# Folding the norm into a linear attention: the new x's sum of squares put together from three sums, and x updated in pairs of tiles

## What is computed

```python
# end of first_block
h = rms_norm(x, norm_ffn_pre_g[l])
f = (jax.nn.silu(h @ w_gate[l]) * (h @ w_up[l])) @ w_down[l]
x = x + rms_norm(f, norm_ffn_post_g[l])
# start of second_block
mod = (cond @ w_ada[l] + b_ada[l])[:, None, :]
sh1, sc1, g1, sh2, sc2, g2 = jnp.split(mod, N_MOD, axis=-1)
h = rms_norm_2(x, norm1_g[l]) * (1 + sc1) + sh1
proj = h @ w_in[l]
gq, gk, gv, gr, glr, aq, ak, av = jnp.split(proj, split_at, axis=-1)
```

## Time and profile before

| | |
|---|---|
| Median of 3 runs | 1440.65 us (1437.36 to 1441.19) |
| The profiled execution | 1441.32 us, of which its span is 1439.3 us |
| PE busy | 1390.4 us, 97% of the span |
| DVE busy | 882.9 us, 61% |
| ACT busy | 590.0 us, 41% |
| Share of the chain that ended last | PE 90%, DVE 5%, ACT 2% |
| DMA moved | 146.72 MB, 102 GB/s on average |

### The profile page before, as it was taken

One profiled execution on the slowest core, in us unless ns is written; L12 is line 12 of the kernel. 1 busy time (PEld: TensorE's weight loads), 2 busy tenths in 40 slices (PEclk: granted clock), 3 DMA queues, 4 the chain that ended last, 5 costly groups with the idle time before them and its releaser, 6 DMA issues.

```text
span 1439.3 us, 18374 instructions
## 1 busy us (share of the span) xinstructions
PE 1390.4 (97%) x6330; PEld 1098.6 (76%) x6330; DVE 882.9 (61%) x1450; ACT 590.0 (41%) x966; POOL 70.5 (5%) x128
## 2 busy tenths in 40 slices
PE   7999999999999999999997999899989999999999
PEld 5777777767768888888884788677668888888887
DVE  5666677777567777774336688666556656655222
ACT  5455445543352323323224524466445444444221
POOL 4000000000001221211000000000000000000000
PEclk9999999999999999999998999999999999999999
DMA  5222212213216565565431122021112232223332
GB/s 186 100 73 74 74 59 78 77 54 114 99 44 201 187 196 192 187 195 160 136 109 59 44 74 74 30 74 59 55 60 77 97 102 87 102 96 107 103 95 84
DMA packets 42319, 146.72 MB, mean 102 GB/s; under 512 B 5392, under 2 KB 5664, under 8 KB 42272
## 3 DMA queue, kind: packets, MB, share of 16 engines
q1 hardware_dynamic: 34448, 120.39, 25.5%
q0 software_dynamic: 7824, 25.70, 5.4%
HBM read 143.97 MB, written 2.10 MB: 101 GB/s over the span
## 4 chain that ended last, share of the span: by engine, by line
PE 90%; DVE 5%; ACT 2%; issue 1%; DMA 0%; DVEq 0%; ACTq 0%
PE bank L598 62%; PE bank L713 12%; PE bank L670 3%; PE bank L633 3%; PE bank L735 2%; PE bank L754 1%; PE bank L923 1%; PE bank L772 1%; ACT w_hi L1079 1%; PE bank L620 1%; DVE w_lo L1549 1%; PE bank L639 1%; DVE gate_last L1739 0%; DVE gate_a L1739 0%; PE bank L775 0%
## 5 line engine op out<-in xcount | busy, mean ns | idle before, releaser
L1549 DVE TENSOR_TENSOR w_lo<-raw,w_hi 128x1024 fp32r<-128x1024 f32 (+1 forms) x225 | 272.2, 1212 | 176.1 <-ACT w_hi L1079 175.3
L1079 ACT ACTIVATE w_hi<-raw 128x1024 fp32r<-128x1024 f32 (+1 forms) x225 | 233.6, 1039 | 302.8 <-PE bank L598 282.0
L598 PE MATMUL bank<-h_hi,w_hi 128*128 128x512 f32 x872 | 346.3, 397 | 0.8 <-DVE gyf L2045 0.8
L598 PE MATMUL bank<-h_hi,w_lo 128*128 128x512 f32 x872 | 340.6, 391 | 0.0
L598 PE MATMUL bank<-h_lo,w_hi 128*128 128x512 f32 x872 | 340.5, 391 | 0.0
L598 PEld LDWEIGHTS bank<-h_hi,w_hi 128*128 128x128 f32 x872 | 164.2, 188 | 42.5 <-issue 7.7
L598 PEld LDWEIGHTS bank<-h_hi,w_lo 128*128 128x128 f32 x872 | 164.3, 188 | 34.6
L598 PEld LDWEIGHTS bank<-h_lo,w_hi 128*128 128x128 f32 x872 | 164.4, 188 | 34.2 <-issue 1.2
L598 PE MATMUL bank<-f_hi,w_lo 128*128 128x512 f32 x352 | 136.9, 389 | 0.0
L598 PE MATMUL bank<-f_hi,w_hi 128*128 128x512 f32 x352 | 136.9, 389 | 0.0
L598 PE MATMUL bank<-f_lo,w_hi 128*128 128x512 f32 x352 | 136.9, 389 | 0.0
(11 more groups left out here) (299 smaller groups left out, 1867.7 us busy)
## 6 DMA issues: line engine op xcount, KB each, us to landing
raw<-in_w_up SPq DMA_DIRECT2D x66, 512.0 KB, 3.2
raw<-in_w_mix SPq DMA_DIRECT2D x48, 512.0 KB, 3.2
ada<-in_w_ada POOLq DMA_DIRECT2D x96, 256.0 KB, 3.2
raw<-in_w_down SPq DMA_DIRECT2D x32, 512.0 KB, 3.5
raw<-in_w_in SPq DMA_DIRECT2D x25, 512.0 KB, 3.3
raw<-in_w_gate SPq DMA_DIRECT2D x22, 512.0 KB, 3.3
raw<-in_w_out SPq DMA_DIRECT2D x16, 512.0 KB, 3.3
raw<-in_w_down SPq DMA_DIRECT2D x16, 384.0 KB, 3.3
```

The costliest lines, as they stand in the source:

```text
L598: last = pe.matmul(to[:, :], wt[:, slot, k, :], act_[:, rhs0 + k, :], start=(k == first and n == 0), stop=(k == K - 1 and n == 2))
L1079: act.activation(w_hi[:, s, 0:K, :], raw[:, s, 0:K, :], ACT.Copy).then_inc(hi_ready[s], 1)
L1549: dve.tensor_tensor(w_lo[:, s, 0:K, :], raw[:, s, 0:K, :], w_hi[:, s, 0:K, :].bitcast(F32), ALU.subtract).then_inc(split_ready[s], 1)
```

## The change

The sum of squares of the new x is no longer taken from the new x. With f the down product, g its gain and r its inverse root, x_new = x + r*g*f, and so

sum(x_new^2) = sum(x^2) + 2 r sum(x*g*f) + r^2 sum((g*f)^2).

The first sum is in bank S0 since the feed-forward norm. The other two are gathered while the down projection runs: per output tile ACT writes `oT` with the gain in it and squares it with the gain (`gained_tile`, three operations in place of two), and DVE makes one product and two additions more (`add_cross`). PE adds three sums over the first seven tiles between the second and third slot of the last output tile (`sums_so_far`, one of them in place of the one after the last product) and three over the last tile behind it (`last_sums`). DVE puts the sums together in four operations, ACT makes the second inverse root of them, and DVE then updates x two tiles at a time (two operations on 1024 elements per pair) between the modulated tiles (`modulated_with_update`). `post_norm` is no longer called here, nor are `new_x_squares` and `sum_squares_by_tile`. The last pair of output tiles is written out of the loop on PE. `split_lo(2)` and the clearing of `gacc` with its `m2_free` stand behind `modulated_with_update`; before, they stood between `post_norm` and `modulated_lo`.

```diff
-        (oT,), _ = region(h_at, ("oT", [KD, S], F32))
+        (oT, cross, cross_sum, gained_sq), h_end = region(
+            h_at, ("oT", [KD, S], F32), ("cross", [2, S], F32), ("cross_sum", [2, S], F32), ("gained_sq", [2, S], F32))
+        assert h_end <= h_at + 2 * KD * S * 4
...
-            def sum_squares_by_tile():
-
-                for k in range(KD):
-                    pe.wait_ge(sq_g[k % 2], w.next(sq_g[k % 2]))
-                    pe.matmul(S0[:, :], ones[:, :], sq[:, k % 2, :], start=(k == 0),
-                              stop=(k == KD - 1)).then_inc(sq_used[k % 2] if k < KD - 1 else ms_ready, 1)
-                for g in range(2):
-                    w.skip(sq_used[g], 4)
...
-            def down(read):
+            def sums_so_far():
+
+                w.skip(sq_g[0], 4)
+                w.skip(sq_used[1], 4)
+                pe.wait_ge(sq_used[0], w.next(sq_used[0], times=4))
+                pe.matmul(S1[:, :], ones[:, :], sqacc[:, :], start=True, stop=False)
+                pe.wait_ge(gained_used[0], 5)
+                pe.wait_ge(gained_used[1], 4)
+                for m in range(2):
+                    pe.matmul(TB[m][:, :], ones[:, :], cross_sum[:, m, :], start=True, stop=False)
+
+            def last_sums():
+
+                pe.wait_ge(sq_g[1], w.next(sq_g[1], times=4))
+                pe.matmul(S1[:, :], ones[:, :], sq[:, 1, :], start=False, stop=True).then_inc(ms_ready, 1)
+                pe.wait_ge(gained_sq_r[1], 4)
+                pe.matmul(T1[:, :], ones[:, :], gained_sq[:, 1, :], start=False, stop=True)
+                pe.wait_ge(cross_r, 1)
+                pe.matmul(T0[:, :], ones[:, :], cross[:, 1, :], start=False, stop=True).then_inc(cross_ms, 1)
+
+            def down(read, sums=None):
                 pe.wait_ge(f_ready, w.next(f_ready, times=NF - 1))

-                def pair(late=None):
+                def pair(late=None, sums=None):
                     for g in range(2):
                         pe.wait_ge(read[g], w.next(read[g], ahead=1))
                         unit(OB[g], 1, f_hi, f_lo, rhs0=8, K=NF)
                         unit(OB[g], 0, f_hi, f_lo, K=NF, first=-1)
+                        if g and sums:
+                            sums()
                         products(OB[g], 2, f_hi, f_lo, 0, 6, rhs0=16, K=6, first=-1,
                                  late=None if g else late).then_inc(unit_done[2], 1)

                 pair(f_ready)
-                with w.repeat(3, {**{split_ready[s]: 2 for s in range(3)}, (read[0], 1): 1, (read[1], 1): 1}):
+                with w.repeat(2, {**{split_ready[s]: 2 for s in range(3)}, (read[0], 1): 1, (read[1], 1): 1}):
                     pair()
+                pair(sums=sums)

             for g in range(2):
                 pe.wait_ge(g_free[g], 23)
             two_tiles(m_hi, m_lo, drained, 3, fresh=mix_ready)
             sum_squares()
             ffn(gate_read, up_read, True)
-            down(drained)
-            sum_squares()
-
-
-            sum_squares_by_tile()
+            down(drained, sums_so_far)
+            last_sums()
+
+
             two_units((S1, G1), (1, 0))
...
+            def gained_tile(g, c):
+
+                gain = col("norm_ffn_post_g", c)
+                act.wait_ge(gained_used[g], w.next(gained_used[g], ahead=1))
+                act.wait_ge(sq_used[g], w.next(sq_used[g], ahead=1))
+                act.activation(sq[:, g, :], OB[g][:, :], ACT.Square).then_inc(sq_g[g], 1)
+                act.activation(oT[:, bass.ds(c, 1), :].rearrange("p a s -> p (a s)"), OB[g][:, :], ACT.Identity,
+                               scale=gain).then_inc(gained[g], 1)
+                act.activation(gained_sq[:, g, :], OB[g][:, :], ACT.Square, scale=gain).then_inc(gained_sq_r[g], 1)
+                act.wait_ge(gained_sq_r[g], w.next(gained_sq_r[g]))
+                act.sem_inc(drained[g], 1)
...
-            down(lambda g, c: out_tile(g, c, oT, OB))
-            inverse_rms()
+            down(gained_tile, {(gained_used[0], 1): 1, (gained_used[1], 1): 1, gained_sq_r[0]: 1, gained_sq_r[1]: 1})
+            inverse_rms(sums=S1)
             split_hi(2)
-            new_x_squares()
-
-
-            inverse_rms()
+            act.wait_ge(ms2_ready, 1)
+            then(act.activation(sqacc[:, :], sqacc[:, :], ACT.Ln, scale=1.0 / D, bias=eps6[:, :]))
+            act.activation(sqacc[:, :], sqacc[:, :], ACT.Exp, scale=-0.5).then_inc(rstd2_ready, 1)
             modulated_hi(lambda k: mod_a[:, 0, k:k + 1], lambda k: modc[:, k:k + 1])
...
+            def modulated(k, root):
+
+                dve.wait_ge(h_ready, w.next(h_ready, ahead=2))
+                dve.tensor_tensor(hbuf[:, k % 2, :], xT[:, k, :], root[:, :], ALU.mult).then_inc(xr_ready, 1)
+
+            def remainder(k):
+
+                dve.wait_ge(n_hi, w.next(n_hi))
+                dve.tensor_tensor(h_lo[:, k, :], hbuf[:, k % 2, :], h_hi[:, k, :].bitcast(F32),
+                                  ALU.subtract).then_inc(h_ready, 1)
+
             def modulated_lo():

                 dve.wait_ge(rstd_ready, w.next(rstd_ready))
-
-                def lo(k):
-                    dve.wait_ge(n_hi, w.next(n_hi))
-                    dve.tensor_tensor(h_lo[:, k, :], hbuf[:, k % 2, :], h_hi[:, k, :].bitcast(F32),
-                                      ALU.subtract).then_inc(h_ready, 1)
-
                 for k in range(KD):
-                    dve.wait_ge(h_ready, w.next(h_ready, ahead=2))
-                    dve.tensor_tensor(hbuf[:, k % 2, :], xT[:, k, :], rstd[:, :], ALU.mult).then_inc(xr_ready, 1)
+                    modulated(k, rstd)
                     if k >= 1:
-                        lo(k - 1)
-                lo(KD - 1)
+                        remainder(k - 1)
+                remainder(KD - 1)
+
+            def modulated_with_update():
+
+                def updated(j):
+                    pair = slice(2 * j, 2 * j + 2)
+                    then(dve.tensor_tensor(oT[:, pair, :], oT[:, pair, :], rstd[:, :].rearrange("p (a s) -> p a s", a=1)
+                                           .broadcast_to([P, 2, S]), ALU.mult))
+                    then(dve.tensor_tensor(xT[:, pair, :], xT[:, pair, :], oT[:, pair, :], ALU.add))
+
+                dve.wait_ge(rstd_ready, w.next(rstd_ready))
+                dve.wait_ge(cross_ms, 1)
+                then(dve.tensor_tensor(sqacc[:, :], T1[:, :], rstd[:, :], ALU.mult))
+                then(dve.scalar_tensor_tensor(out=sqacc[:, :], in0=T0[:, :], scalar=2.0, in1=sqacc[:, :], op0=ALU.mult,
+                                              op1=ALU.add))
+                then(dve.tensor_tensor(sqacc[:, :], sqacc[:, :], rstd[:, :], ALU.mult))
+                dve.tensor_tensor(sqacc[:, :], sqacc[:, :], S0[:, :], ALU.add).then_inc(ms2_ready, 1)
+                updated(0)
+                dve.wait_ge(rstd2_ready, 1)
+                modulated(0, sqacc)
+                modulated(1, sqacc)
+                for j in range(1, 4):
+                    updated(j)
+                    for k in (2 * j, 2 * j + 1):
+                        remainder(k - 2)
+                        modulated(k, sqacc)
+                remainder(KD - 2)
+                remainder(KD - 1)

...
+            then(dve.memset(cross_sum[:, :, :], 0.0))
+
+            def add_cross(g, c):
+
+                dve.wait_ge(gained[g], w.next(gained[g]))
+                then(dve.tensor_tensor(cross[:, g, :], at_k(xT, c), at_k(oT, c), ALU.mult))
+                then(dve.tensor_tensor(cross_sum[:, 0, :], cross_sum[:, 0, :], cross[:, g, :], ALU.add))
+                dve.wait_ge(gained_sq_r[g], w.next(gained_sq_r[g]))
+                dve.tensor_tensor(cross_sum[:, 1, :], cross_sum[:, 1, :], gained_sq[:, g, :], ALU.add).then_inc(gained_used[g], 1)
+
+            def last_cross():
+
+                skip_last_square()
+                dve.wait_ge(gained[1], w.next(gained[1]))
+                dve.tensor_tensor(cross[:, 1, :], xT[:, 7, :], oT[:, 7, :], ALU.mult).then_inc(cross_r, 1)
+
             def square_and_modulation(g, c):

                 add_squares(g)
+                add_cross(g, c)
...
-            post_norm(oT, lambda k: col("norm_ffn_post_g", k))
+            modulated_with_update()
             split_lo(2)
             dve.memset(gacc[:, :, :], 0.0).then_inc(m2_free, 1)


-            modulated_lo()
             for n in (2, 3, 4):
```

More of the change, by code:

```diff
@@ L1324, in _ @@
             out_tile(1, 7, oT_mix, G)
-            def new_x_squares():
-                for k in range(KD):
-                    act.wait_ge(x_ready, w.next(x_ready))
-                    square(k, xT[:, k, :])
             inverse_rms()
@@ L1356, in _, with down @@
             w.start(unit_done, "down")
-            def down(each):
+            def down(each, more):
                 split_hi(2, K=6)
                 per = {**{raw_in[s]: 2 for s in range(3)}, **{(unit_done[s], 1): 2 for s in range(3)}, unit_done[2]: 2,
-                       (sq_used[0], 1): 1, (sq_used[1], 1): 1}
```

(1 more changed line is left out.)

25 lines of the change are left out of this document (15 added, 10 removed).

## The result

The changed kernel takes **1446.36 us** (median of 7 runs, 1445.41 to 1447.03) against 1441.19 (median of 7, 1437.36 to 1442.87) for the kernel before: +5.2 us, a ratio of 1.0035, 95% interval 1.0024 to 1.0046. The profiled execution took 1445.6 us, 1443.7 of it span. The median is 1.3 us above the forecast of 1445.1. The prediction took 0.3% as what can be told from no change: the ratio is just beyond that, and its interval reaches across it.

What follows compares the result with a forecast made beforehand. PE, busy 97%, bounds, with a near-equal ACT and DVE path from 801.72 to 826.74 us. Of loads 16.7 us late 4.1 come through: 1445.4 from the execution's 1441.3, 1444.8 from the median, written 1445.1; range 1443.5 to 1447.5.

Steps and rivals of the forecast that it cites:

- First combining operation: DVE, behind the down projection: the last tile's sums can be read, and combining starts, at 774.0 us.
- The three sums: PE, end of the down projection: three sums ahead of the last slot, with no pause to cover them, +2.58 us.
- GLA products: PE, GLA projection: products begin at 784.0 us, 4.6 us earlier, then wait for tiles that come every 2.6 us.
- Last remainder: DVE, end of update and modulation: the last remainder starts at 797.9 us, behind ACT's work on the last tile.
- The update's pace: DVE, update and modulation: each of three further pairs takes 5.18 us, together 15.5 us, to 796.1.
- `m2_free`: DVE's clearing of `gacc`, now behind the update: comes at 801.9 in place of 785.2 us, 16.7 us later, holding SP's loads.
- Tile 2 at ACT: ACT's rounding of tile 2 waits for its late load until 805.8 us, where it started at 801.72: +4.1 us.
- Small products: PE, GLA stage: start at 830.8 us, 826.74 plus 4.1, after a pause of 2 to 3 us.
- the rival with a lost clock: PE pauses before `z` (gate product; 2.5 us slack) and small products: half clock costs 2.2 us; 1447.3 us, chance 0.15.
- Both clock rivals: Same delay: clock given back near 920 us, 3 us back, 1442.1, chance 0.25; or clock lost, 1447.3, chance 0.15.
- The faster rival: Loads in time, and the GLA products' 4.6 us earlier start reaches the end; 1436.1 us, chance 0.08.
- The slow update: DVE's update: an operand repeated over two tiles halves the rate, 4.9 us more in all; 1450 us, chance 0.05.

Runs made afterwards that it cites:

- e3: The changed kernel with SP's load of `wgate` issued ahead of its wait for `m2_free`, the tiles still behind it; 1447.02 us, ratio 1.0044 to the kernel before.
- e4: The kernel before with only the split of tile 1 and the clearing of `gacc` moved behind `modulated_lo`; 1444.21 us, ratio 1.0021.
- e7: The changed kernel with four more sums on PE filling its pause ahead of `z`, the gate product; 1450.17 us, ratio 1.0048 to the kernel before.
- e1: The changed kernel with the clearing of `gacc` (and its `m2_free`) put ahead of `modulated_with_update`; 1439.77 us, ratio 0.9988 to the kernel before.
- e10: e1 with the three early sums moved behind the last product and the inverse-root scaling left out for tiles 2 to 7; 1435.71 us, ratio 0.9963.
- e1 to e3: e1, e3 and, between them, the changed kernel with loads of tiles 2 and 3 issued before SP's wait for `m2_free`: 1446.83 us, ratio 1.0037.
- e12: The same kernel as e1, run on another chip; 1441.60 us, ratio 1.0006 to the kernel before.
- e8: e6 with the scaling and addition that update x for tiles 4 to 7 moved from DVE to GpSimd; 1443.04 us, ratio 1.0006.
- e6: e1 with `gacc` cleared by GpSimd, behind DVE's last cross product, in place of DVE; 1439.82 us, ratio 0.9987 to the kernel before.

## Why the prediction was right

By its own steps, with the 0.7 us of the execution's own lateness taken off (forecast, then measured):

- First combining operation 774.0; 774.04. Four operations to 776.9; 776.9. The three sums: 2.58 us ahead of the last slot; 2.58.
- GLA products from 784.0; 783.9. Last remainder from 797.9; 797.75. The update's pace, three times 5.18 us, is in the chain to the hundredth: 784.52, 789.70, 794.87 are the starts of a pair's first multiplication.
- `m2_free` 801.9; 801.7. `wgate` 803.6; 803.5. Tile 2 at ACT 805.8, **+4.1 us**; 805.76, **+4.0**. The wait of ACT for the load is the one that was named, and its 5.67 us is the "about 5" of the last part.
- Small products 830.8; 832.2. Here 1.4 us are missing.

The term that was mis-sized is the clock behind the pause for `wgate`. The half clock fell ahead of `z`, where the rival with a lost clock had put one of its two pauses. That rival counted 2.2 us for it, "covered by 2.5 us of slack". PE ran at half clock from 804 to 814 us, and it cost 1.8 us in `z` and 2.8 in the unit behind it, 4.5 in all. The slack was even larger than forecast. Without this loss PE would have been through the first unit at 812.0, and ACT wanted it at 815.3: 3.3 us. At the small products it was the same 3.3 (PE at 828.3, DVE's mask at 831.6). (It had been counted as 2.5 with four units at 5.67 us; the three behind the first took 5.4 each.) 4.5 less 3.3 is about the 1.26 us that ACT waited for the unit, and this is nearly all of the missing 1.4: from the rounding of tile 2 to DVE's split of tile 4 after took 818.16 - 806.49 = 11.67 us, before 811.97 - 801.72 = 10.25. The pause of "2 to 3 us" at the small products was eaten by the slower PE, so nothing was lost behind it; e3, e4 and e7 show that loss, where PE came in time.

Both clock rivals happened in part in one execution: 1.4 us lost in front, and 1.7 given back in the stretches behind 920 us. The forecast for the profiled execution, 1445.4, met 1445.6 because these two and the 0.7 at the start nearly cancel: that closeness is luck. For the medians the shift is 5.2 us, 1.1 over the 4.1 of the mechanism.

The faster rival needed the clearing to end by 797.8 and DVE to hand over a tile in 1.4 us. e1 supplies the first and e10 goes some way to the second: with the first alone the kernel is about level with before, and with the sums behind and three of the update's eight long operations gone it is 0.37% faster. The slow update is refuted: an operand repeated over two tiles ran at 1.22 us for 1024 elements. In the mechanism, then, the prediction is shown by e1 to e3, and by e4 for the delay at the small products; that the change without its late clearing would be level with before, it had not worked out.

## What to carry to other kernels

When work moves ahead of an instruction that frees a buffer, price what that instruction starts before pricing the work: here the update on DVE only took the place of what it removed (e1 and e12 are level with before), and a clearing of 1.8 us behind it, with the loads that waited for it, cost 5. Where slack is to cover a pause, price the half clock that can follow it as well as the pause: here 3.3 us of slack would have covered the 2.2 that were counted, and not the 4.5 that came. And a step moved off the path is worth what its new place has of cover: of the 2.58 us that three sums took ahead of the last slot, 2.2 came back when they stood behind it.

## What the runs showed of the hardware

GpSimd and DVE held each other up. Operations with two operands in the same memory took up to 2.29 us on DVE (1.23 without GpSimd) and 2.24 on GpSimd (1.3 at its quickest) while both ran (e8), so four tiles moved to GpSimd made the first GLA product later; a DVE operation with one of its operands in a bank was not held (0.69 us). A clearing on GpSimd, which reads nothing, held a DVE operation on 8 elements for 1.74 us (e6). The Trainium skill, "SBUF — State Buffer", section "Who interferes with whom", has it that the two share a pair of ports and that whoever comes first keeps it for the whole instruction; e8 agrees, and e6 agrees if that operation on one operand runs in a mode with two ports, which no run here shows.

The clock at short pauses is not a property of the kernel: behind a pause of 2.1 us it was full in e1 and half in e12, the same kernel. Nor does the longer pause cost more: behind 4.52 us (e3) the small products ran at half clock and the stretch from 836 us at full clock; behind 3.35 us (e7) 10.2 us ran at half. So such a loss is best carried as a range, 0 to 5 us by these runs, at each pause that stands ahead of packed work.
